# Four U gathers and then the four V gathers of a set, in place of one and one in turn

## The chip, the cores and the metric

The kernel runs on one core of one Trainium2 chip. The metric is the device time of one execution in microseconds (us). A gather here is one indirect DMA of 128 rows of 4 KB, 512 KB in all; U and V are the two expert tables.

## The reference, cut to what matters

One layer: a mixer (an mLSTM and a stick-breaking attention, 4 and 8 heads, over 9 tiles of 128 tokens), then a feed-forward with experts picked by product keys, for 8 tiles of 128 tokens. The gathers serve the second part:

```python
def block(xt):                                   # one tile of 128 tokens
    q = (xt @ w_query).reshape(T, Hh, 2, PEER_HALF)              # Hh = 8 heads
    s = jnp.einsum('thpc,pnc->thpn', q, sub_keys)
    sv, si = lax.top_k(s, K)                                     # K = 16
    cand = (sv[:, :, 0, :, None] + sv[:, :, 1, None, :]).reshape(T, Hh, K * K)
    cidx = (si[:, :, 0, :, None] * N_KEYS + si[:, :, 1, None, :]).reshape(T, Hh, K * K)
    fv, fi = lax.top_k(cand, K)
    eidx = jnp.take_along_axis(cidx, fi, axis=-1)                # 16 of 16384 experts
    g = jax.nn.softmax(fv, axis=-1)
    ue, ve = expert_u[eidx], expert_v[eidx]                      # rows of 1024 floats
    act = jax.nn.gelu(jnp.einsum('td,thkd->thk', xt, ue), approximate=False)
    return jnp.einsum('thk,thkd->td', g * act, ve)
```

So each of 64 heads (8 tiles by 8 heads) needs 16 gathers from `expert_u` and 16 from `expert_v`: 2048 gathers, 1074 MB.

## The kernel before, in words

The first 600 us or so project the tokens and fold the query weights with the keys. Behind that, all engines walk through the same program of slots, 16 slots to a head. In slot `o` of head G each engine does a fixed list, in its own order:

- POOL issues the gathers, and nothing else. `gather_u(G, k)` fetches row k of U for each of 128 tokens into one of 4 ring slots (`RING_U`); before it issues, it waits until VectorE (DVE) has done the dot product that used that ring slot, which is U gather n-4 (`dotted`). `gather_v(G - 1, k)` fetches for the head before into a ring of 8 slots, two sets of four (`SET`); only the first gather of a set waits, for PE to have summed the set two back (`summed_sets`). The V gathers of a head follow one head later since their weights need the finished dots.
- DVE does `dot(G, o)` (L1250) at the start of slot o when U gather o has landed, and after it a part of the routing of a later head: the top 16 of the scores in slots 6, 7, 9 and 10 (`best_halves` L1149 first), the indices in slots 11 to 13; in slots 1 and 2 the weights of the head before; and parts of the mixer of the next tile.
- PE in slots 0, 4, 8 and 12 starts with `sum_set` (16 matmuls, L1351 into `acc`), for the V set of which the last gather was issued just before U gather o. In slot 4, behind it, comes `scores` (16 matmuls, L1351 into `bank` from `n2T`), which `best_halves` in DVE's slot 6 waits for. The mixer's matmuls follow in the same slots.
- ACT copies and does the mixer's and the softmax's exponentials; SP issues plain loads and stores.

An engine can't pass over an instruction that waits: what stands behind it in its program waits too. For DVE that means that a dot stands behind a top-8 that waits for PE, and for POOL that all gathers stand behind one that waits for a dot.

Of the kernel before, what the change touches and what calls it, by code (L numbers as in the profile page):

```python
# [38 lines left out]
PH, TOPK, NKEY = 8, 16, 128  # L39
# [7 lines left out]
SET = 4  # L47
# [20 lines left out]
def wait(eng, sem, value):  # L68

    if isinstance(value, int) and value <= 0:  # L70
        return
    eng.wait_ge(sem, value)
# [17 lines left out]
def tile_of_head(G):  # L90

    return G // PH + 1
# [33 lines left out]
def program(nc, xT, xn_in, w_in, w_out, w_queryT, sub_t, mlstm_w, gain_cols, g_final,  # L126
            gate_bias, expert_u, expert_v, out):
    with ExitStack() as ctx:
# [170 lines left out]
        def b2(i):  # L299
# [6 lines left out]
        COLS = [("u", 0, MIX), ("ks", 2056, MIX), ("qs", 1544, MIX), ("v", 512, MIX),  # L306
                ("so", 1024, MIX), ("vs", 2568, MIX), ("gates", 1536, 2 * MH)]
        w_landed = {n: sem(f"w_landed_{n}") for n, _, _ in COLS}
        x_landed = [sem(f"x_landed{i}") for i in range(2)]
        squared, summed, rs_ready, n_ready = sem("squared"), sem("summed"), sem("rs_ready"), sem("n_ready")  # L310
        unit_done = {n: sem(f"{n}_done") for n, _, _ in COLS}
        unit_taken = {n: sem(f"{n}_taken") for n, _, _ in COLS}
        conv_ready, conv_exp, hist_moved = sem("conv_ready"), sem("conv_exp"), sem("hist_moved")
        staged_act, staged_dve = sem("staged_act"), sem("staged_dve")
# [210 lines left out]
        @block.gpsimd  # L525
        def _(pool):
            def select(tile, sign, op, fill_value):

                pool.affine_select(out=tile[:, :], in_=tile[:, :], compare_op=op, fill=fill_value, base=0,
                                   pattern=[[-sign, P]], channel_multiplier=sign).then_inc(fills, 1)  # L530

            for tile, value in ((ident, 1.0), (ident_h, 1.0), (neg_m, 0.0), (neg_s, 0.0), (before, 1.0),
                                (neg_tri, -1.0), (ones, 1.0), (tri, 1.0), (valid, 1.0),
                                (invalid, 0.0), (eps, EPS), (one, 1.0)):
                pool.memset(tile[:, :], value)
            pool.memset(neg_blk[:, :, :], -1.0)
            pool.memset(lw[:, :], 0.0)
            pool.iota(iota_i[:, :], [[1, TOPK]], base=0, channel_multiplier=0)
            pool.memset(state[:, :, :], 0.0).then_inc(fill, 1)
            pool.wait_ge(fill, 1)  # L540
            select(ident, 1, ALU.is_equal, 0.0)
            select(ident_h, 1, ALU.is_equal, 0.0)
            select(neg_m, -1, ALU.is_ge, NEG)
            select(neg_s, -1, ALU.is_gt, NEG)
            select(before, -1, ALU.is_gt, 0.0)
            select(neg_tri, 1, ALU.is_ge, 0.0)
            select(tri, -1, ALU.is_ge, 0.0)

            pool.affine_select(out=valid[:, :], in_=valid[:, :], compare_op=ALU.is_ge, fill=0.0,
                               base=-(P - N_META), pattern=[[0, 1]], channel_multiplier=1).then_inc(fills, 1)  # L550
            pool.affine_select(out=invalid[:, :], in_=invalid[:, :], compare_op=ALU.is_ge, fill=NEG,
                               base=-(P - N_META), pattern=[[0, 1]], channel_multiplier=1).then_inc(fills, 1)
            pool.affine_select(out=neg_blk[:, :, :], in_=neg_blk[:, :, :], compare_op=ALU.is_equal, fill=0.0,
                               base=0, pattern=[[-1, MH], [0, P]], channel_multiplier=1).then_inc(fills, 1)
            pool.tensor_copy(iota16[:, :], iota_i[:, :]).then_inc(fills, 1)


            def gather_u(G, k):

                T, h = tile_of_head(G), G % PH  # L560
                n = G * TOPK + k
                s = n % RING_U
                wait(pool, dotted, n - RING_U + 1)
                pool.indirect_dma_start(out=ring_u[:, s, :], out_offset=None, in_=expert_u,  # L564
                                        in_offset=bass.IndirectOffsetOnAxis(
                                            ap=chosen[T % 2][:, h * TOPK + k:h * TOPK + k + 1], axis=0)
                                        ).then_inc(u_landed[s], 16)

            def gather_v(G, k):

                T, h = tile_of_head(G), G % PH
                n = G * SET + k // SET
                r, c = k // SET, k % SET
                col = h * TOPK + SET * c + r
                if c == 0:
                    wait(pool, summed_sets, n - 1)
                pool.indirect_dma_start(out=ring_v[:, n % 2 * SET + c, :], out_offset=None, in_=expert_v,  # L577
                                        in_offset=bass.IndirectOffsetOnAxis(ap=idx_v[T % 2][:, col:col + 1], axis=0)
                                        ).then_inc(v_landed[n % 2], 16)

            for G in range(HEADS + 1):
                if G < HEADS:
                    pool.wait_ge(idx_ready, G + 1)
                if G > 0:
                    pool.wait_ge(idx_v_ready, G)
                for k in range(TOPK):
                    if G < HEADS:
                        gather_u(G, k)
                    if G > 0:
                        gather_v(G - 1, k)  # L590


        @block.scalar
# [1107 lines left out]
```

## Time and profile before

| | us |
|---|---|
| median of 3 runs | 3823.41 |
| lowest, highest | 3808.22, 3844.6 |
| profiled execution | 3818.86 |
| its span | 3817.1 |

| engine | busy us | share of the span |
|---|---|---|
| PE | 2173.3 | 57% |
| DVE | 2208.0 | 58% |
| ACT | 614.4 | 16% |
| POOL | 2285.0 | 60% |

The page's part 2 gives the DMA engines as 9 tenths busy or more in nearly every fortieth of the span from 667 us on, and the chain that ended last is POOL for 39%, PE for 19% and DVE for 9%. A share of busy time counts an instruction only while it runs: POOL's time between two gathers isn't in its 60%.

### The profile page before, as it was taken

Reading aid. Unit: us, or ns where it says so; the run is one execution under the profiler, and the core shown is the slowest. Engines: PE = TensorE matmul, PEld = TensorE weight load, DVE = VectorE, ACT = ScalarE, POOL = GpSimd, SP = SyncE. Lnnn points to the kernel's source line nnn. Section 1 sums busy time; section 2 is a strip of 40 time slices with the busy share of each in tenths; the row PEclk is TensorE's granted clock in tenths of the full one; section 3 lists DMA queues with packets and bytes.
Section 4 is the critical chain, followed back from the end, with each engine's and each line's share of the span. In section 5 each row is a group of like instructions: output and inputs, shape, how many; then the busy total and the mean of one; then the engine's idle time right before and its main releaser. Section 6 shows DMA issues by size and latency. Waiting matters only on the chain.

```text
span 3817.1 us, 32434 instructions
## 1 busy us (share of the span) xinstructions
PE 2173.3 (57%) x10710; PEld 1136.1 (30%) x10710; DVE 2208.0 (58%) x5450; ACT 614.4 (16%) x1254; POOL 2285.0 (60%) x2079
## 2 busy tenths in 40 slices
PE   7999864544465445553665457545664477433333
PEld 6777653211232122221332123212321233111100
DVE  2333326666675656665766666657666666666552
ACT  0000122101121112110221023101311132100000
POOL 0000003777677776777677767677677667777675
PEclk9999877765777667666777678766876688666656
DMA  5111414999999999999899989998999899999998
GB/s 178 45 44 38 166 34 137 355 360 374 338 356 339 376 350 346 342 378 348 318 367 374 367 330 345 363 350 323 335 364 374 331 337 362 348 363 369 351 360 315
DMA packets 342724, 1169.34 MB, mean 306 GB/s; under 512 B 37124, under 2 KB 51108, under 8 KB 341544
## 3 DMA queue, kind: packets, MB, share of 16 engines
q0 software_dynamic: 294912, 1073.87, 75.5%
q1 hardware_dynamic: 47656, 93.56, 6.9%
q8 instruction: 77, 1.26, 0.1%
q14 instruction: 79, 0.65, 0.0%
HBM read 1145.25 MB, written 22.04 MB: 306 GB/s over the span
## 4 chain that ended last, share of the span: by engine, by line
POOL 39%; PE 19%; issue 16%; DVE 9%; another core or an unknown queue 8%; DMA 8%; ACT 2%; SPq 0%; POOLq 0%; DVEq 0%; ACTq 0%
POOL work L577 20%; POOL work L564 19%; PE bank L1351 16%; DMA work<-expert_u,chosen 5%; DVE work L1250 3%; PE acc L1351 3%; DMA work<-expert_v,idx_v 2%; DVE work L878 1%; DVE work L886 1%; DVE rest L1153 0%; ACT work L724 0%; ACT work L721 0%; DVE sri L1152 0%; ACT work L728 0%
## 5 line engine op out<-in xcount | busy, mean ns | idle before, releaser
L564 POOL DMA_INDIRECT work<-expert_u,chosen x1024 | 1107.5, 1082 | 1127.4 <-DVE chosen L886 597.5
L1250 DVE CUSTOM_DVE_ANT_0 work<-work,xs 128x1024 f32<-128x1024 f32 x1024 | 1249.3, 1225 | 844.0 <-DMA work<-expert_u,chosen 773.6
L577 POOL DMA_INDIRECT work<-expert_v,idx_v x1024 | 1171.7, 1144 | 388.0 <-issue 308.7
L1351 PE MATMUL acc<-work,lw 128*32 128x512 f32 x4096 | 801.3, 912 | 1013.7 <-DMA work<-expert_v,idx_v 948.2
L1351 PEld LDWEIGHTS acc<-work,lw 128*32 128x32 f32 x4096 | 144.7, 143 | 1419.8 <-DMA work<-expert_v,idx_v 801.1
L1351 PE MATMUL bank<-weights,work 128*128 128x512 f32 x672 | 296.0, 598 | 1.3 <-issue 1.3
L1351 PE MATMUL bank<-weights,n2T 128*128 128x256 f32 x1024 | 256.6, 405 | 1.7 <-issue 1.3
L1351 PE MATMUL bank<-work 64*128 64x128 f32 (+4 forms) x1610 | 212.9, 304 | 50.3 <-DVEq L1178 26.1
L1351 PEld LDWEIGHTS bank<-weights,n2T 128*128 128x128 f32 x1024 | 202.9, 205 | 121.5 <-issue 94.4
L1351 PEld LDWEIGHTS bank<-work 128*128 128x128 f32 (+1 forms) x1610 | 198.6, 211 | 96.9 <-issue 78.3
L1351 PE MATMUL bank<-work,weights 128*128 128x128 f32 x1664 | 192.2, 278 | 3.1 <-DVE work L886 3.1
L1351 PEld LDWEIGHTS bank<-work,weights 128*128 128x128 f32 x1664 | 190.1, 194 | 3.4 <-DVE work L886 3.4
L1351 PE MATMUL bank<-which_eight,c_spread 128*128 128x16 f32 x128 | 33.2, 338 | 264.5 <-DVE c_spread L878 239.3
L1351 PEld LDWEIGHTS bank<-weights,work 128*128 128x128 f32 x672 | 127.4, 192 | 158.8 <-issue 158.4
L1351 PE MATMUL bank<-work,neg_tri 128*128 128x512 f32 x176 | 121.4, 779 | 91.1 <-DVE work L886 65.0
L784 ACT ACTIVATE gate<-best_h,neg_top 128x16 f32<-128x16 f32 x64 | 19.3, 301 | 698.9 <-DVE neg_top L882 642.5
L1351 PEld LDWEIGHTS bank<-which_eight,c_spread 128*128 128x128 f32 x128 | 27.6, 265 | 341.7 <-DVE c_spread L878 293.2
L886 DVE SCALAR_TENSOR_TENSOR work<-work,gains 128x128 f32<-128x128 f32 x180 | 50.5, 346 | 106.4 <-ACT work L614 105.5
L1590 PE MATMUL bank<-ident,w_spread 128*128 128x128 f32 x64 | 25.8, 404 | 140.8 <-DVE w_spread L878 98.0
L886 DVE SCALAR_TENSOR_TENSOR work<-bank,work 128x512 f32<-128x512 f32 x88 | 56.7, 685 | 82.4 <-ACT work L728 61.2
L878 DVE TENSOR_TENSOR work<-work 128x512 f32<-128x512 f32 (+2 forms) x102 | 63.6, 654 | 65.9 <-PE bank L1351 55.0
L1351 PE MATMUL bank<-work,ones 128*128 128x512 f32 (+2 forms) x162 | 100.1, 704 | 0.0
(187 smaller groups left out, 2043.5 us busy)
## 6 DMA issues: line engine op xcount, KB each, us to landing
work<-kv_dram SPq DMA_DIRECT2D x88, 256.0 KB
work<-expert_u,chosen POOLq DMA_INDIRECT x1024
work<-expert_v,idx_v POOLq DMA_INDIRECT x1024
weights<-w_in SPq DMA_DIRECT2D x6, 2048.0 KB, 17.4
mix_dram<-work SPq DMA_DIRECT2D x8, 1024.0 KB, 4.0
weights<-w_queryT SPq DMA_DIRECT2D x4, 2048.0 KB, 17.1
work<-xT SPq DMA_DIRECT2D x9, 512.0 KB, 6.8
kv_dram<-work SPq DMA_DIRECT2D x9, 512.0 KB, 5.7
```

The source lines that it names most:

```text
L564: pool.indirect_dma_start(out=ring_u[:, s, :], out_offset=None, in_=expert_u, in_offset=bass.IndirectOffsetOnAxis(ap=chosen[T % 2][:, h * ...
L577: pool.indirect_dma_start(out=ring_v[:, n % 2 * SET + c, :], out_offset=None, in_=expert_v, in_offset=bass.IndirectOffsetOnAxis(ap=idx_v[T ...
L784: nc.scalar.activation(gate[T % 2][:, a:a + TOPK], best_h[:, :], ACT.Exp, bias=neg_top[:, :], accum_out=gate_sum[T % 2][:, G % PH:G % PH + ...
L878: return nc.vector.tensor_tensor(out_, a, b, op)
L886: return nc.vector.scalar_tensor_tensor(out=out_, in0=a, scalar=s, in1=b, op0=op0, op1=op1)
L1250: nc.vector.tensor_tensor_reduce(s, s, xs[T % 2][:, :], 1.0, 0.0, ALU.mult, ALU.add, dots[:, col:col + 1]).then_inc(dotted, 1)
L1351: return nc.tensor.matmul(out_, lhsT, rhs, start=start, stop=stop, skip_group_check=True)
L1590: nc.tensor.transpose(bank[6][:, 320:448], w_spread[:, :], ident[:, :]).then_inc(w_turned, 1)
```

## The change

In POOL's loop over the heads, the inner loop over the 16 gathers becomes one over four rounds. A round issues four U gathers, then the four V gathers of one set. The number of gathers, their waits' values, the rings and every other engine's program stay.

```diff
-                for k in range(TOPK):
+                for r in range(TOPK // SET):
                     if G < HEADS:
-                        gather_u(G, k)
+                        for k in range(SET * r, SET * r + SET):
+                            gather_u(G, k)
                     if G > 0:
-                        gather_v(G - 1, k)
+                        for k in range(SET * r, SET * r + SET):
+                            gather_v(G - 1, k)
```

POOL's program in the middle of a head, before (`expert_u` and `expert_v` are the tables, `chosen` and `idx_v` the indices, `work` holds both rings):

```order
L564 DMA work<-expert_u,chosen 128x1024 [waits dotted]
L577 DMA work<-expert_v,idx_v 128x1024 [waits summed_sets]
L564 DMA work<-expert_u,chosen 128x1024 [waits dotted]
L577 DMA work<-expert_v,idx_v 128x1024
L564 DMA work<-expert_u,chosen 128x1024 [waits dotted]
L577 DMA work<-expert_v,idx_v 128x1024
L564 DMA work<-expert_u,chosen 128x1024 [waits dotted]
L577 DMA work<-expert_v,idx_v 128x1024
L564 DMA work<-expert_u,chosen 128x1024 [waits dotted,idx_v_ready,idx_ready]
```

The same stretch in the changed kernel, with the round ahead and the first of the next head:

```order
L564 DMA work<-expert_u,chosen 128x1024 [waits dotted] x4
L577 DMA work<-expert_v,idx_v 128x1024 [waits summed_sets]
L577 DMA work<-expert_v,idx_v 128x1024 x3
L564 DMA work<-expert_u,chosen 128x1024 [waits dotted,idx_v_ready,idx_ready]
L564 DMA work<-expert_u,chosen 128x1024 [waits dotted] x3
L577 DMA work<-expert_v,idx_v 128x1024 [waits summed_sets]
L577 DMA work<-expert_v,idx_v 128x1024 x3
```

The waits stay with their gathers. A U gather still stands eight gathers behind the one whose ring slot it takes over; the first V gather of a set, which waits for PE, now stands behind four U gathers of its round in place of one. The last V gather of a set stands right before the next round's first U gather, as it did.

DVE's program is the same before and after. Its slots 5 to 9, with a dot at the start of each (`work,dots<-work,xs`), are in both:

```order
L1250 ISA work,dots<-work,xs 128x1024 [waits u_landed1]
L1250 ISA dots 128x1
L1250 ISA work,dots<-work,xs 128x1024 [waits u_landed2]
L1250 ISA dots 128x1
L1149 MAX srt<-bank 128x8 [waits scores_done]
L1149 MAX srt<-bank 128x8
L1152 MAX_INDEX sri<-srt,bank 128x8 [waits dve_t]
L1153 MATCH_REPLACE rest<-srt,bank 128x128
L1152 MAX_INDEX sri<-srt,bank 128x8
L1153 MATCH_REPLACE rest<-srt,bank 128x128
L878 TENSOR_TENSOR work<-bank,work 128x512 [waits wexp_ready,dve_t]
L1250 ISA work,dots<-work,xs 128x1024 [waits u_landed3]
```

What moves against it is the landing of U: four in a row, then none while four V gathers land.

## Rows read from the trace of the kernel before

**Rows 1.** Who waited for whom on POOL, whole run: total, times, longest

```profile
POOL work L577 <- issue: 308.7, 984, 3.4
POOL work L564 <- issue: 295.6, 946, 1.7
POOL work L564 <- DVE dots L1250: 234.3, 77, 12.7
```

**Rows 2.** The page's part 5: POOL's two groups, busy and mean ns

```profile
L564 POOL DMA_INDIRECT work<-expert_u,chosen x1024 | 1107.5, 1082 | 1127.4 <-DVE chosen L886 597.5
...
L577 POOL DMA_INDIRECT work<-expert_v,idx_v x1024 | 1171.7, 1144 | 388.0 <-issue 308.7
```

**Rows 3.** Four stretches: length, busy time of engines, PE clock, DMA share, GB/s

```profile
660.00:3817.00 3157.00, 1639.65 (x7672) 727.81 (x7672) 1973.47 (x4893) 522.59 (x1067) 2257.00 (x2030) 0.70 0.95 352
...
2425.00:2430.00 5.00, 5.00 (x24) 1.66 (x23) 4.27 (x19) 0.00 (x0) 1.03 (x2) 1.00 0.69 280
...
2465.00:2475.00 10.00, 7.72 (x32) 3.99 (x32) 4.50 (x12) 0.57 (x3) 7.80 (x8) 0.76 1.02 409
...
3500.00:3700.00 200.00, 76.76 (x345) 25.57 (x341) 117.64 (x299) 16.13 (x30) 143.81 (x134) 0.62 0.95 352
```

**Rows 4.** Timeline (start, duration, engine, line): `best_halves`, dots 7 to 13, a gather

```profile
2425.44 0.50 DVE L1149 MAX8 srt<-bank 128x8 f32<-128x128 f32 x2 [6.71 <-remote]
...
2427.16 1.22 DVE L1250 CUSTOM_DVE_ANT_0 work<-work,xs 128x1024 f32<-128x1024 f32 x1
...
2429.64 1.23 DVE L1250 CUSTOM_DVE_ANT_0 work<-work,xs 128x1024 f32<-128x1024 f32 x1 [0.19 <-DVE sri L1162]
2429.91 1.77 POOL L577 DMA_INDIRECT work<-expert_v,idx_v  x1 [0.30 <-issue]
2430.79 1.22 DVE L1250 CUSTOM_DVE_ANT_0 work<-work,xs 128x1024 f32<-128x1024 f32 x1
...
2433.77 1.23 DVE L1250 CUSTOM_DVE_ANT_0 work<-work,xs 128x1024 f32<-128x1024 f32 x1
...
2435.91 1.23 DVE L1250 CUSTOM_DVE_ANT_0 work<-work,xs 128x1024 f32<-128x1024 f32 x1
...
2439.39 1.22 DVE L1250 CUSTOM_DVE_ANT_0 work<-work,xs 128x1024 f32<-128x1024 f32 x1
...
2442.10 1.22 DVE L1250 CUSTOM_DVE_ANT_0 work<-work,xs 128x1024 f32<-128x1024 f32 x1
```

**Rows 5.** Timeline, first and last of 536 pairs: U gather, then its dot

```profile
673.24 0.94 POOL L564 DMA_INDIRECT work<-expert_u,chosen  x1 [0.30 <-issue]
...
679.23 1.23 DVE L1250 CUSTOM_DVE_ANT_0 work<-work,xs 128x1024 f32<-128x1024 f32 x1 [0.88 <-DMA work<-expert_u,chosen]
...
3771.62 1.00 POOL L564 DMA_INDIRECT work<-expert_u,chosen  x1 [0.31 <-issue]
...
3778.22 1.23 DVE L1250 CUSTOM_DVE_ANT_0 work<-work,xs 128x1024 f32<-128x1024 f32 x1 [1.29 <-DMA work<-expert_u,chosen]
```

**Rows 6.** Timeline, first and last of 61 heads: dot 4, then `best_halves`

```profile
677.12 1.22 DVE L1250 CUSTOM_DVE_ANT_0 work<-work,xs 128x1024 f32<-128x1024 f32 x1
...
686.75 0.49 DVE L1149 MAX8 srt<-bank 128x8 f32<-128x128 f32 x2
...
3654.74 1.23 DVE L1250 CUSTOM_DVE_ANT_0 work<-work,xs 128x1024 f32<-128x1024 f32 x1 [1.29 <-DMA work<-expert_u,chosen]
...
3662.25 0.50 DVE L1149 MAX8 srt<-bank 128x8 f32<-128x128 f32 x2 [1.16 <-PE bank L1351]
```

**Rows 7.** Timeline, PE: one `sum_set`, and one `scores`

```profile
2411.01 3.64 PE L1351 MATMUL acc<-work,lw 128*32 128x512 f32 x16 [3.25 <-DMA work<-expert_v,idx_v]
...
2414.58 4.02 PE L1351 MATMUL bank<-weights,n2T 128*128 128x256 f32 x16
```

**Rows 8.** Timeline, POOL: a U gather of the first head

```profile
621.66 4.83 POOL L564 DMA_INDIRECT work<-expert_u,chosen  x1 [12.70 <-DVE dots L1250]
```

**Rows 9.** Groups by line: `best_halves`' first operation; busy, mean ns, idle before it

```profile
L1149 DVE MAX8 srt<-bank 128x8 f32<-128x128 f32 x128 | 31.6, 288 | 101.4 <-remote 71.2 <-PE bank L1351 29.9 <-issue 0.2
```

## The prediction

> **What bounds the kernel now.** I read POOL first, since all traffic behind 600 us starts there. Its waits [rows 1] and its two groups [rows 2] add up: 1107.5 + 1171.7 = 2279 us of gathers, 309 + 296 = 604 us of gaps of 0.30 us between them, and 234 us in which a U gather waits for a dot. That is 3117 of the 3157 us behind 660 us [rows 3]. So POOL is never free, though the page calls it 60% busy.
>
> A gather needs 0.94 us where nothing is in its way [rows 5], with the gap 1.24. The means are 1.08 and 1.14 [rows 2]. The excess, 2279 - 2048 x 0.94 = 354 us, comes from DVE's dots: a V gather that starts 0.27 us into a dot takes 1.77 us [rows 4], 0.83 more, which is the rest of that dot, and it gets in between this dot and the next, that follows without a gap. I call this the lock.
>
> Are the DMA engines the limit? They moved 352 GB/s over the long stretch, but 409 over 10 us in which POOL ran freely, and 280 after a stall of POOL [rows 3]. A gather costs them 0.524 MB / 409 = 1.28 us, POOL 1.24: close, but POOL's delays decide.
>
> From the start of a U gather to its dot, where DVE stood waiting, it takes 6.25 us: the median of 536 pairs, of which the first and last have 5.99 and 6.60 [rows 5].
>
> One head takes (3771.62 - 673.24) / 1002 x 16 = 49.5 us [rows 5]: 32 x 1.24 = 39.7 bare, 354/64 = 5.5 lock, 234/64 = 3.7 waits for dots, the rest for V.
>
> **The change, part by part.** No gather, byte or instruction is added. What changes is when U lands: four in about 5 us, then none for 5 us, where it was one each 3.1 us. The distance from a U gather to the reuse of its slot stays eight gathers. Four terms follow.
>
> (a) The wait of a V set for PE is looser by three gathers. It was nearly nothing; I give 0.6 us a head for it, from the rest in the account above.
>
> (b) The tail. The last U gather is issued three gathers earlier, 3.7 us once. Left out.
>
> (c) The lock. In a burst of light slots dots follow landings at 1.24 to 1.28 us, about POOL's own step, so after one collision (0.6 us on average, half a dot) POOL falls into the gaps. Where slots carry routing, dots stand 2 to 3 us apart and each meets a gather again.
>
> (d) The scores. This is what turns it. PE starts `sum_set` of slot 4 when the last V of the set has landed, just before U4 lands in both orders; then come `scores`. In one head they took 3.64 + 4.02 = 7.7 us [rows 7]. `best_halves` starts 9.63 us after dot 4 in the first head and 7.51 in the last [rows 6]; over 61 heads the mean is 9.0, the median 8.4. Before, U7 lands 9 us after U4, so dot 7 behind `best_halves` is about on time. Now U7 lands 3.8 us after U4, and its dot must still wait for 9.0 + 1.72 = 10.7 us (1.72 is from `best_halves` to dot 7 [rows 4]). The U gather that needs dot 7's slot, U11, is due at POOL some 8 us after U4 has landed, and is held back, with four V gathers behind it.
>
> Worked through for a head, with U4 issued at time 0, landing 6.25 after issue, DVE's steps from dot to dot as [rows 4] has them (slot 7 2.48, slot 8 1.15, slot 9 2.98, slot 10 2.14, slot 12 2.71 us) and 1.24 a gather:
> - U4 to V7: 0 to 9.9, one collision, so U8 at 10.6, U9 11.8, U10 13.1; U11 would be at 14.3.
> - `best_halves` at 6.25 + 9.0 = 15.25, dot 7 at 17.0, done 18.2; U11 at 18.4: 4.1 us late.
> - DVE: dots 8, 9, 10, 11 at 19.45, 20.6, 23.6, 25.7. V8 starts at 19.7 and is locked to 20.55, V9 21.8, V10 23.0, V11 24.3 locked to 24.7, U12 26.0 locked to 26.8.
> - U13 to V15: 28.1 to 35.5. Dots 12 to 15 at 33.05, 35.8, 37.5, 38.7. U16 36.9, U17 locked to 38.6, U18 39.9, U19 41.1, V16 42.3, V17 locked to 44.25, V18 locked to 46.0, V19 47.3, U20 48.5.
>
> So 48.5 us a head: 39.7 + 4.1 late + 4.7 lock. Before, the same account has 39.7 + 5.5 and the waits. Two things must be added. Of the 234 us of waits for dots (3.7 a head) a part is term (d) in its old size, and the rest comes from the mixer's work and stays. No row parts them; with all of it (d) nothing is added, with none 3.7. I take half, 1.9. And the mixer now meets a DVE that does its first slots of a round close together, sooner than PE can answer: between nothing (if every such wait falls into the pause behind the round's last dot) and 1.8 us a head. The upper end is the mixer's own DVE work taken whole: DVE is busy for 0.625 of the long stretch and for 0.588 of 200 us in which no mixer runs [rows 3], and 0.037 x 49.5 = 1.8. I take 0.7, nearer to nothing, since each round has 5 us of pause. 48.5 + 1.9 + 0.7 = 51.1, against 49.5: **+1.6 us a head**. (a) is already in it, since 48.5 has no V wait.
>
> 63 heads have both kinds: 63 x 1.6 = 101 us. On the profiled execution's own time, 3818.9 (the span and 1.8 around it, and 4.5 under the median of the runs), that gives 3920 us, 2.6% more.
>
> **A rule that speaks against any change.** The 10 us at 409 GB/s [rows 3] say that the memory can give more than the mean of 352. The Trainium skill, "DMA: Bandwidth & Descriptors", Specifications, puts the limit of HBM for one core at about 358 GB/s. By that rule the kernel would stand at the limit, and the order of gathers would be worth nothing: 3820 us. The trace doesn't agree in a short stretch; it doesn't show a long one.
>
> **The rivals.**
> - *Slower by the late dot 7*, as above: 0.62.
> - *No change*, since the DMA engines are the true limit and POOL's delays only follow. For it: a DMA share of 0.95 [rows 3]. Against it: bytes and share both fall after a stall of POOL (280 GB/s, 0.69), and free gathers take 0.94 with no back-pressure. Within 1%, around 3820; together with the case that terms (c) and (d) cancel: 0.23.
> - *Faster by the lock.* If the dots of all rounds fall into POOL's step, the lock is 4 x 0.8 = 3.2 us a head, not 5.5, and the V wait goes. That decides where `best_halves` starts less than some 5.6 us after U4 lands: then dot 7 isn't late. It would give 39.7 + 3.2 + 3.7 = 46.6, 2.9 us less a head, 3636 us; with half of it 3730. For it: PE's granted clock averages 0.70 [rows 3], between its levels of 1.2 and 2.4 GHz, so the two steps are shorter in some heads than the 7.7 us of [rows 7]. Against it: a mean of 9.0 over 61 heads. 0.13.
> - *POOL starved.* One gather took 4.83 us with three dots behind each other running [rows 8]. If a burst of four dots kept POOL out for its whole length, each round would cost 4 x 1.15 - 0.6 = 4 us more: 252 rounds, 1000 us, 4900 us. Against it: the V gather at 2429.91 that got in between two such dots [rows 4]. 0.02.
>
> **How the numbers follow.** Each us of `best_halves`' start is one us a head, 63 us in all. With the median 8.4 the forecast is 3882; with 7.0, 3794. With the mixer's 1.8 whole it is 3920 + 69 = 3989, and with two thirds of the 1.8 that the halved 3.7 leaves open on top, 4065. The likeliest case alone spans 3790 to 4065. The whole range reaches a little into the faster case: 3770 to 4065. About 1% is what a measurement of this kernel tells from no change. Faster by over 1%: 0.13; within: 0.23; slower, the starved case with it: 0.64.
>
> **What would show it.** POOL's waits for dots should grow from 234 us to some 450, in more than 100 waits, and most of them at U11; its two groups should fall from 2279 us together to about 2230 (4.7 against 5.5 of lock). DVE's wait of L1149 for PE [rows 9] should grow from 101 us to over 250. DMA bytes stay and the mean falls from 352 to about 342 GB/s. Wrong if L1149 waits longer and L564 doesn't: then dot 7 has slack that I don't see. Wrong too if the mean gather grows past 1.2 us: that would be the lock, not the scores.

## The result, and the profile after

The changed kernel takes 3956.8 us, the median of four runs (3947.1 to 3962.0), against 3827.2 for the kernel before in the same comparison: a ratio of 1.034, 95% interval 1.028 to 1.039. The profiled execution has a span of 3952.9 us, 135.8 more than before (3817.1). The forecast was 3920 us, slower, by the late dot 7.

POOL's waits in the kernel after (who waited for whom: total, times, longest), against [rows 1]:

```profile
POOL work L564 <- DVE dots L1252: 465.8, 123, 12.7
POOL work L577 <- issue: 309.5, 1015, 0.3
POOL work L564 <- issue: 287.0, 900, 2.1
POOL work L577 <- PE acc L1353: 9.9, 6, 4.7
POOL work L577 <- remote: 7.4, 3, 3.8
```

Two waits of the kernel before that [rows 1] doesn't have, the V gathers' for `sum_set`:

```profile
POOL work L577 <- remote: 68.9, 34, 3.4
POOL work L577 <- PE acc L1351: 10.4, 6, 3.6
```

POOL's two groups in the page's part 5 of the kernel after (busy, mean ns, idle time ahead of them), against [rows 2]:

```profile
L564 POOL DMA_INDIRECT work<-expert_u,chosen x1024 | 1077.4, 1052 | 1348.4 <-DVE chosen L888 595.7
...
L577 POOL DMA_INDIRECT work<-expert_v,idx_v x1024 | 1177.3, 1150 | 326.8 <-issue 309.5
```

The first operation of `best_halves` in the kernel after, by line, against [rows 9], and the long stretch, against [rows 3]:

```profile
L1151 DVE MAX8 srt<-bank 128x8 f32<-128x128 f32 x128 | 31.8, 290 | 233.2 <-remote 143.3 <-PE bank L1353 73.2 <-issue 16.7
```

```profile
660.00:3952.00 3292.00, 1643.94 (x7665) 728.15 (x7664) 1957.43 (x4890) 520.10 (x1065) 2232.59 (x2030) 0.69 0.91 337
```

(Lines behind the change are two higher than before: L1250 is now L1252.) POOL's groups give the whole account. U gathers: idle ahead of them 1348.4 against 1127.4, that is +221.0; V gathers: 326.8 against 388.0, -61.2; busy time 2254.7 against 2279.2, -24.5. The sum is +135.3, for 135.8 of span. The waits for dots grew by 231.5 us; the V gathers' waits for `sum_set`, 79 us before (the page calls most of them "remote"), fell to 17. The DMA engines' share fell from 0.95 to 0.91 and the rate from 352 to 337 GB/s: they have more idle time, so they are not what bounds the changed kernel.

Sorted by the U gather that waits, and counted over the usual gap of 0.30 us (my sums from the timeline), U11 waited 62.7 us in 23 heads before and 212.8 us in 53 heads after. The others together, the first head's among them, went from 148.5 to 216 us. Most of that rise stands in few heads: U10 50.9 us in 10 heads (28.1 in 9 before), U6 23 in 8 (2 before), U2 19 in 7 (0.4 before), those of U10 and U2 all one to three heads into a tile of eight (heads 1, 2, 9, 10, 17, 18, 19 and so on).

One round of the changed kernel shows it step by step. This is its timeline in an execution on another chip (the run after2, below): start, duration, engine, line.

```profile
2512.06 0.94 POOL L564 DMA_INDIRECT work<-expert_u,chosen  x1 [0.30 <-issue]
...
2522.06 0.94 POOL L564 DMA_INDIRECT work<-expert_u,chosen  x1 [0.30 <-issue]
2524.80 0.94 POOL L564 DMA_INDIRECT work<-expert_u,chosen  x1 [1.81 <-DVE dots L1252]
2526.05 0.94 POOL L577 DMA_INDIRECT work<-expert_v,idx_v  x1 [0.30 <-issue]
```

```profile
2517.23 1.23 DVE L1252 CUSTOM_DVE_ANT_0 work<-work,xs 128x1024 f32<-128x1024 f32 x1
...
2521.58 0.50 DVE L1151 MAX8 srt<-bank 128x8 f32<-128x128 f32 x2 [3.12 <-PE bank L1353]
...
2523.30 1.23 DVE L1252 CUSTOM_DVE_ANT_0 work<-work,xs 128x1024 f32<-128x1024 f32 x1
```

```profile
2513.20 3.64 PE L1353 MATMUL acc<-work,lw 128*32 128x512 f32 x16 [6.76 <-DMA work<-expert_v,idx_v]
2516.78 4.77 PE L1353 MATMUL bank<-weights,n2T 128*128 128x256 f32 x16
```

U7 is issued at 2512.06. In this run a dot for which DVE stood waiting starts 6.45 us after its gather (median of 269), so U7's rows land near 2518.5, just as dot 6 (2517.23) ends. But PE began `sum_set` only at 2513.20 and the scores end at 2521.55. `best_halves` starts at 2521.58 and dot 7 at 2523.30, some 5 us after its data. U11, due at 2523.3 as well, must wait for the end of that dot and goes out at 2524.80, with four V gathers behind it.

### The profile page after: what moved, and what is told of

Read it like the earlier page. It is cut to its first block, busy times and chain, and to the rows that moved or that the text cites. A ratio compares the mean times of both kernels' runs of the same rounds, so it can differ in the third digit from the quotient of the medians.

```text
span 3952.9 us, 32434 instructions
## 1 busy us (share of the span) xinstructions
PE 2176.9 (55%) x10710; PEld 1135.8 (29%) x10710; DVE 2194.1 (56%) x5450; ACT 613.4 (16%) x1254; POOL 2260.5 (57%) x2079
## 4 chain that ended last, share of the span: by engine, by line
POOL 31%; PE 23%; issue 13%; DVE 12%; DMA 12%; another core or an unknown queue 7%; ACT 3%; SPq 0%; POOLq 0%; DVEq 0%; ACTq 0%
PE bank L1353 18%; POOL work L577 17%; POOL work L564 13%; DMA work<-expert_v,idx_v 6%; DVE work L1252 6%; DMA work<-expert_u,chosen 6%; PE acc L1353 5%; DVE work L880 1%; DVE rest L1155 1%; DVE sri L1154 1%; DVE srt L1151 1%; DVE work L888 1%; ACT work L726 0%; ACT work L723 0%
## 5 line engine op out<-in xcount | busy, mean ns | idle before, releaser
L564 POOL DMA_INDIRECT work<-expert_u,chosen x1024 | 1077.4, 1052 | 1348.4 <-DVE chosen L888 595.7
L1252 DVE CUSTOM_DVE_ANT_0 work<-work,xs 128x1024 f32<-128x1024 f32 x1024 | 1242.4, 1223 | 794.5 <-DMA work<-expert_u,chosen 730.3
L577 POOL DMA_INDIRECT work<-expert_v,idx_v x1024 | 1177.3, 1150 | 326.8 <-issue 309.5
L1353 PE MATMUL bank<-weights,n2T 128*128 128x256 f32 x1024 | 267.5, 418 | 1.3 <-issue 0.8
L1353 PEld LDWEIGHTS bank<-weights,n2T 128*128 128x128 f32 x1024 | 211.1, 213 | 124.7 <-issue 94.6
L1151 DVE MAX8 srt<-bank 128x8 f32<-128x128 f32 x128 | 31.8, 290 | 233.2 <-remote 143.3
L738 ACT ACTIVATE work<-bank 128x512 f32<-128x512 f32 x88 | 52.3, 597 | 380.2 <-PE bank L1353 260.3
```

The lines of the kernel that those rows point to most:

```text
L738: nc.scalar.activation(zl[hg], bank[2 + hg][:, :], ACT.Exp).then_inc(a_ready, 1)
L1151: last = nc.vector.max(values[:, 0:8], src)
L1252: nc.vector.tensor_tensor_reduce(s, s, xs[T % 2][:, :], 1.0, 0.0, ALU.mult, ALU.add, dots[:, col:col + 1]).then_inc(dotted, 1)
L1353: return nc.tensor.matmul(out_, lhsT, rhs, start=start, stop=stop, skip_group_check=True)
```

## The experiments

Each run stands beside the kernel before on its own chip, and three chips were met: A, where before takes 3799 us, B with 3647 and C with 3645. So ratios are compared, and traces only of one chip; where a comparison crosses chips, I say so. Which chip the result was taken on isn't known. The kernel before took 3827 us there and DVE's waits look like A's (last section), so the traces of the result are set beside A's. X is the mean time from the start of dot 4 to that of `best_halves` over 60 heads, from the timelines.

### The cost of the scores itself

a_few, in `scores`, chip A:

```
-                for k in range(KC):
+                for k in range(2):
...
-                              w_score[:, 2 * h:2 * h + 2, k, :], k == 0, k == KC - 1)
+                              w_score[:, 2 * h:2 * h + 2, k, :], k == 0, k == 1)
```

> The changed kernel with 4 of the 16 matmuls of scores (2 of 8 parts of the sum over the model's width are computed, the other 6 left out, so other experts are picked, as many as before). Scores are ready up to 3 us earlier, best_halves stays in slot 6. Late-dot-7 theory: each us is a us a head while dot 7 is late, about 50 heads: U11's waits fall from 213 to some 80 us, the time to 3800 to 3850 us. DMA theory: 3940 to 3970 us.

Measured: 3822.3 us, 1.005 (1.001 to 1.009). X fell from 8.8 to 6.5 us, U11's waits from 212.8 to 123.7 us. POOL in a_few:

```profile
POOL work L564 <- DVE dots L1252: 340.2, 105, 8.9
```

The kernel leaves out three quarters of the scores' matmuls, and the time came as the theory says; U11's waits fell less than to its 80 us. The direction fits over three runs of this order (two chips): X is 8.8, 7.0 and 6.5 us, and U11 waits 213, 121 and 124 us. Yet that alone doesn't say that the order makes them dear. The control is b_few, the same edit in the kernel before, chip B.

> The kernel before, with 4 of the 16 matmuls that make a head's scores (so the scores are incomplete); it is the control for the same cut in the changed kernel, which brought that one from 3957 to 3822 us. Theory (the late scores cost time through the order of the gathers, since dot 7 holds back U11 with four V gathers behind it): in the order before they cost little, so this gives 3760 to 3800 us, 0 to 40 us less than before, dotted waits from 234 to about 170 us. Rival (PE's work for the scores costs the same whatever the order of the gathers, by its clock or its place on the chain): a gain of 100 us or more here too, below 3700 us.

Measured: 3592.6 us, 0.983 (0.979 to 0.986); waits for dots 94.5 us in 49. That is between theory and rival: the kernel before pays 1.7% for its scores too, more than I had given it. The cut takes 2.9 points from the changed kernel and 1.7 from the one before (on different chips), so some 1.1 of the 3.4 points are the scores made dearer by the order. That is a difference of four measured times; their intervals together leave it open by about 0.7 either way. What stands between the two with few scores is still 2.3 points.

### best_halves behind dot 7

a_late moves two steps of `routing` in the changed kernel, chip A; b_late does it in the one before.

```
-                if o == 6:
+                if o == 7:
                     best_halves(G)
-                if o == 7:
+                if o == 8:
                     next_halves(G)
```

> The changed kernel, with DVE's best_halves moved from slot 6 to slot 7, so behind dot 7, the last of its round, and next_halves to slot 8. PE and the gathers stay. Late-dot-7 theory: U11 no longer waits for a dot that stands behind the wait for the scores; its 213 us of waits go nearly whole, POOL's waits for dots fall from 466 to under 280 us, and the time from 3957 to 3740 to 3800 us. DMA theory (bursts of U feed the 16 engines worse): nothing changes there, 3940 to 3970 us. Mixer theory (the waits come from the mixer's ping-pong with PE): at most a fifth of the 130 us comes back, 3925 us or more.

> The kernel before, with the same move of best_halves to slot 7 and next_halves to slot 8. Late-dot-7 theory: the waits of U10 to U12 (110 us of 234) shrink but less is to be had than in the changed kernel: 3750 to 3800 us from 3827. If the move helps for another reason that has nothing to do with the order of gathers (DVE waits less for PE in all), it gives the same number of us in both kernels.

Measured: a_late 3926.2 us, 1.032 (1.028 to 1.036), a miss; b_late 3797.8, 0.998 (0.993 to 1.002), no gain. In b_late POOL's waits for dots are 190.1 us, 44 less than before, but its waits of L577 are 103.4, 24 more. In a_late U11's waits fell from 212.8 to 46.5 us as foretold, but U12 to U15 rose to 250 us in 103 waits:

```profile
POOL work L564 <- DVE dots L1252: 487.0, 163, 12.7
```

The lateness was passed on, not removed. On chip A a second thing confuses the picture: waits of up to 12 us at MAX8 (last section). So I ran the edit again on chip C, with a small memset between the wait and MAX8, as a_late2, beside after2, which is the changed kernel unaltered.

> The changed kernel again, unaltered, so that the other three stand beside it on the same chip; chips differ (the kernel before took 3799 us on one and 3647 us on another). 1.034 of the time of before if the cost of the order doesn't hang on the chip; 1.04 if the faster chip, which loses less elsewhere, shows it more.

> The changed kernel with best_halves in slot 7 and next_halves in slot 8, as in the run that gave 1.032, and with the memset of 8 columns between the wait for the scores and MAX8. Theory (dot 7 ahead of best_halves frees U11; what spoiled it in the first run were waits of 5 to 12 us for scores that PE had finished, which the faster chip doesn't show): 1.00 to 1.02 there, with U11's dotted waits under 20 us. Rival (the lateness only passes to dots 8 to 11 and so to U12 to U15, on any chip): 1.03 again. On a chip with the long waits: if they stand ahead of the memset, PE's signal is late; if ahead of MAX8, it is MAX8 that can't start.

Measured: after2 3789.8 us, 1.039 (1.036 to 1.042); a_late2 3749.3, 1.029 (1.026 to 1.031). Chip C has no long waits, X is 6.95 for after2, and the order costs no less. POOL's waits for dots in after2, then in a_late2:

```profile
POOL work L564 <- DVE dots L1252: 322.9, 127, 12.6
```

```profile
POOL work L564 <- DVE dots L1253: 362.5, 173, 12.6
```

POOL's groups in after2, then in a_late2:

```profile
L564 POOL DMA_INDIRECT work<-expert_u,chosen x1024 | 1087.9, 1062 | 1192.4 <-DVE chosen L888 595.6
...
L577 POOL DMA_INDIRECT work<-expert_v,idx_v x1024 | 1164.7, 1137 | 321.3 <-issue 310.5
```

```profile
L564 POOL DMA_INDIRECT work<-expert_u,chosen x1024 | 1051.0, 1026 | 1223.5 <-DVE chosen L888 598.1
...
L577 POOL DMA_INDIRECT work<-expert_v,idx_v x1024 | 1121.2, 1095 | 320.0 <-issue 309.9
```

The waits for dots went up, from 322.9 to 362.5 us: U11 fell from 120.6 to 37.9, U14 and U15 rose from 35.8 to 131.5. The gain of 50 us is in the other column: 80 us less busy time of POOL. In after2 649 gathers took over 1.00 us, in a_late2 503, so fewer met a dot; a_late, without the memset, has 70 us less busy time than the kernel after, and b_late only 6 less than the one before. The rival is right on the waits, on both chips: `best_halves` then stands ahead of dots 8 to 11, which are drawn together as well.

### The fifth slot

a_ring5 in the changed kernel, chip A (the last gain is left out to make room):

```
-RING_U = 4
+RING_U = 5
```

> The changed kernel with 5 U ring slots in place of 4. Room for it comes from leaving out the final gain: the output is scaled by itself instead, same operation and size, and one load of 512 KB at the start is gone. U11 then needs dot 6, which stands ahead of best_halves, and U12 needs dot 7. Late-dot-7 theory: the waits at U11 go, some come back at U12; POOL's waits for dots under 200 us, 3700 to 3800 us. DMA theory: a gather more in flight, at most 20 to 40 us less.

Measured: 3832.9 us, 1.009 (1.005 to 1.013), less gain than expected. Waits for dots are still 330.4 us in 128, now the most at U12 (89.2), the gather that needs dot 7's slot in a ring of five. The control b_ring5, chip B:

> The kernel before with five U slots in place of four, the last gain left out to make room (the output is scaled by itself in its place); it is the control for the same change of the changed kernel, which came to 3833 us. Theory (the ring of U binds POOL only where the order puts four U gathers behind a late dot): the order before needs the fifth slot less, some 50 to 100 of the 234 us of dotted waits go, 3700 to 3770 us. Rival (POOL's own issue of 1072 gathers, or the transfer rate, is what bounds both): 3780 to 3800 us, with the time that leaves the dotted waits found in other waits of POOL or in longer gathers.

Measured: 3593.5 us, 0.984 (0.982 to 0.987), waits for dots 65.1 us in 23. The theory's 3700 to 3770 us were written for chip A; as shares of before they are 0.974 to 0.992, and that held. A fifth slot gives the changed kernel 2.5 points and the one before 1.6. So it brings the orders only from 3.4 to 2.4 points apart (on different chips, and open by about 0.7 either way). The fifth slot doesn't take the late dot away: in the changed kernel dot 7 now holds back U12. This run alone doesn't say how large its part is. POOL's waits in b_ring5:

```profile
POOL work L562 <- DVE dots L1248: 65.1, 23, 12.0
```

### How large, and where, the groups are

a_two, chip B: in POOL's loop, groups of two U and two V gathers.

```
-                for r in range(TOPK // SET):
+                for r in range(TOPK // 2):
...
-                        for k in range(SET * r, SET * r + SET):
+                        for k in range(2 * r, 2 * r + 2):
```

> The changed kernel with groups of two: two U gathers, then two V gathers, and so on. Theory (what costs is how many U gathers in a row need slots whose dots come late): a U gather behind dot 7 now has two V gathers behind it, and the cost lies between the two orders: 3850 to 3900 us where four give 3957 and one gives 3800; dotted waits about 340 us. Rival (any grouping upsets the stream by the same amount): 3930 to 3960 us. Second rival (the cost comes only of four in a row, a whole ring): 3790 to 3820 us.

Measured: 3682.0 us, 1.009 (1.006 to 1.013), waits for dots 180.2 us in 80, of which U11 49.2. The theory's 3850 to 3900 us are 1.013 to 1.027 of chip A's before, so the cost is a little under its range and above that of the second rival: it grows faster than the group. A group of four is also a whole ring of U; no run parts the two. POOL's waits in a_two:

```profile
POOL work L564 <- DVE dots L1252: 180.2, 80, 12.7
```

a_shift, chip C: groups of four, moved by two.

```
-                for r in range(TOPK // SET):
+                for r in range(TOPK // SET + 1):
                     if G < HEADS:
-                        for k in range(SET * r, SET * r + SET):
+                        for k in range(max(SET * r - 2, 0), min(SET * r + 2, TOPK)):
                             gather_u(G, k)
-                    if G > 0:
+                    if G > 0 and r < TOPK // SET:
```

> The changed kernel with the groups of four moved by two: U0 and U1, V set 0, U2 to U5, V set 1, U6 to U9, V set 2, U10 to U13, V set 3, U14 and U15, then the next head. Theory (dots 4 to 7 of one group are drawn together to 1.3 us apart, and the scores, best_halves and dot 7 don't shrink with them, so that dot 7 is late for U11): now the pause between two groups falls between dots 5 and 6, where the scores are worked out anyway, so most of the cost goes: 0.99 to 1.01 of the time of before, dotted waits under 300 us, U11 under 30 of them. Rival (grouping in fours costs by itself, wherever it falls): 1.025 to 1.04 as after. Second rival (it only moves to the next routing step, next_halves in slot 7 and the join in slot 8, now in the middle of a burst): 1.015 to 1.03, with the waits at U12 and U13.

Measured: 3708.4 us, 1.017 (1.015 to 1.020), more than the theory's 0.99 to 1.01, though its two marks came (198.6 us of waits for dots; U11 10.5). Groups of the same size, put so that the pause between two of them falls where the scores are worked out, cost 1.7% in place of 3.9: a little over half of the cost hung on where the bursts fall, and U11's waits alone fell by more (120.6 to 10.5 us) than the span did (84.8 us). The rest is what the second rival named, now small waits over many gathers (U12 33.5 us in 39), and in longer gathers:

```profile
POOL work L564 <- DVE dots L1252: 198.6, 131, 12.6
```

```profile
L564 POOL DMA_INDIRECT work<-expert_u,chosen x1024 | 1094.6, 1069 | 1074.0 <-DVE chosen L888 595.5
L577 POOL DMA_INDIRECT work<-expert_v,idx_v x1024 | 1197.0, 1169 | 317.1 <-issue 311.4
```

### Scores ahead of sum_set

b_swap in the kernel before, chip C: PE does the scores first in slot 4.

```
+                    if o == 4 and 0 <= I - ROUTE < HEADS:
+                        scores(I - ROUTE)
                     if o % SET == 0 and 0 <= v < SETS:
                         sum_set(v)
...
-                        if o == 4:
-                            scores(I - ROUTE)
```

> The kernel before with PE doing a head's scores ahead of the sum_set that stood in front of them, so that they end some 2 to 3.6 us earlier. It is the one edit here that might beat both kernels with the output whole. Theory (dot 7's deadline has slack in the order before, and lateness of the scores still costs part of the dotted waits): 0.99 to 1.00 of the time of before, dotted waits down by 20 to 60 us, best_halves 2 us earlier after dot 4. Rival (sum_set later by 4 us makes a V slot late, and so POOL's V gathers): 1.00 to 1.01, with waits of L577 on PE acc up by 30 us or more.

Measured: 3621.9 us, 0.994 (0.991 to 0.996): faster than both kernels, with the output whole. POOL's waits and groups in b_swap:

```profile
POOL work L564 <- DVE dots L1250: 105.2, 60, 12.7
POOL work L577 <- PE acc L1351: 23.0, 16, 4.1
```

```profile
L564 POOL DMA_INDIRECT work<-expert_u,chosen x1024 | 1080.7, 1055 | 996.1 <-DVE chosen L886 597.4
L577 POOL DMA_INDIRECT work<-expert_v,idx_v x1024 | 1173.0, 1145 | 338.2 <-issue 315.2
```

It also gives a clean account on one chip. Between b_swap and after2 lie 177.9 us of span: U gathers' idle time +196.3, V gathers' -16.9, busy time -1.1. Of the waits for dots, U11 gives 114 us (120.6 against 6.8) and U10 38. (b_swap isn't the kernel before; that one takes 23 us more on this chip, and no trace of it there was taken.)

### What a late MAX8 waits for

a_probe is the changed kernel with a memset between the wait for the scores and MAX8, one execution on chip B:

```
                 dve.wait_ge(scores_done, G + 1)
+                nc.vector.memset(srt[:, 1, 8:16], 0.0)
```

> The changed kernel with one more DVE instruction per head between the wait for the scores and the first MAX8: a memset of 8 columns of the list that MAX8 writes next. In the kernel after, 23 or so of these waits last over 3 us though PE's last scores matmul has ended in the records. If PE's signal comes late (first theory), the memset takes over the long waits and MAX8 follows it within 0.3 us. If it is MAX8 that can't start while POOL issues gathers (second theory), the memset starts when the signal comes, within 1.3 us of the last matmul, and the long waits stand ahead of MAX8. The time stays at 3930 to 3970 us by both.

Measured: 3798.2 us, one execution, 1.04 of its before. It settles nothing on the long waits, since chip B showed none. It couldn't have parted the two theories by the place of the wait either. The memset stands ahead of MAX8 in the program, but in the trace it starts 0.01 us behind it, and all 51 waits (135.0 us) are put down to MAX8:

```profile
789.47 0.28 DVE L1151 MAX8 srt<-bank 128x8 f32<-128x128 f32 x1 [1.89 <-issue]
789.48 0.07 DVE L1175 MEMSET srt<- 128x8 f32 x1
```

The last matmul of these scores ends at 789.42; in all 51 waits MAX8 starts within 0.1 us of it.

## Why the prediction was right

The step that turned it, (d), was right in place and nearly in size. It put U11 4.1 us late in each head; measured are 212.8 / 64 = 3.3, and 4.0 in each of the 53 heads where it waits. The groups of four moved by two took U11's waits away, and over half of the cost with them. The cost came out at 135.8 / 64 = 2.1 us a head, where 1.6 had been forecast. In the prediction's own terms, before and after:

| us a head | forecast | measured |
|---|---|---|
| POOL's waits for dots | 3.7 to 6.7, +3.0 | 3.3 to 6.7, +3.4 |
| (a), V's waits for PE | 0.6 to 0, -0.6 | 1.2 to 0.2, -1.0 |
| (c), the lock | 5.5 to 4.7, -0.8 | 5.5 to 5.1, -0.4 |

The rows add up to +1.6 and +2.0. The errors of the first two cancel, which is luck, and the lock is what is left of the miss. Where each came from:

- U11: 4.1 foretold, 3.3 measured. `best_halves` started 8.8 us after dot 4, not 9.0, and some ten heads have no such wait. The good match is partly luck of the chip: on chip C, where no MAX8 is late, U11 waits 120.6 / 64 = 1.9 us a head and the order costs no less.
- All other waits for dots: 1.9 + 0.7 = 2.6 us a head foretold, 216 / 64 = 3.4 measured, which makes up for U11. The 1.9, a half of the old waits taken for want of a row, stood for what was 148.5 / 64 = 2.3, and the mixer's 0.7 for a rise of 68 us, 1.1. The rise stands mostly in few heads, while the routing has its steps in every head; that the mixer makes it is likely but not shown.
- (a): the prediction took it from the rest of its account of a head, where it came out too small. The 39.7 us already hold the usual gap of 0.30 us ahead of every gather, and the 234 us of waits for dots hold it again, 77 times. Over that gap they are 211 us, and the V gathers' waits 76.
- (c): small, in the right direction, and not fixed by the order: a_late2 shows 80 us less of it. Gathers of over 1.00 us went from 708 to 652.
- The signs: waits for dots 465.8 us in 123 (some 450, over 100), of which U11 is about half and not most; both groups 2254.7 us (about 2230); DVE's wait at L1151 233.2 us (over 250); DMA rate 337 GB/s (342).

The rival that the DMA engines are the limit is out. So is the rule that went with it, which the prediction took as a limit of this core. The Trainium skill ("DMA: Bandwidth & Descriptors", Specifications) gets its about 358 GB/s of HBM for one core by halving a stack's 716 between two cores. This kernel runs on one core, and the trace doesn't agree with 358 as its limit: chip C moved 377 GB/s over 2940 us in b_swap:

```profile
660.00:3600.00 2940.00, 1625.50 (x7658) 749.17 (x7660) 1970.06 (x4889) 518.70 (x1060) 2229.93 (x2030) 0.73 0.99 377
```

There its DMA share is 0.99, so this kernel is now close to both limits, POOL's and the engines'. b_few and b_ring5 are there too (380 and 381 GB/s, share 0.99, from 660 to 3500 us), so the controls in the old order may have had less left to gain than the runs that they stand beside.

Of the whole cost I call this shown: about half hangs on where the bursts fall, with U11's waits behind `best_halves` and its scores as what goes when they are moved (a_shift: 2.1 of 3.9 points). The other half came with grouping in fours even then. The whole grows with the size of the group (0.9 points for two, 3.4 to 3.9 for four). How that other half divides into waits of single steps and locked gathers wasn't parted. Two things would tell more and weren't run: the scores ahead of `sum_set` (b_swap's edit) in the changed kernel, and a trace of the kernel before on chip B or C.

## What to carry to other kernels

Grouping issues for one consumer draws its work together, while the steps that another engine feeds into the same stretch keep their length; so ask of each slot of the ring when its reader must be done, measured in issues of the new order, and what stands between that reader and its data. Where such a step is late, look first at its place against the burst: in the changed kernel a_shift took off 2.1 points, moving the step one slot back 1.0 (a_late2), with longer waits at the next gathers. The producer's own order is worth a trial too: b_swap took 0.6 points off the kernel before, where one slot back (b_late) took nothing clear of noise. And give an ablation its control in the old order: the cut scores looked like the whole answer until the kernel before gained 1.7% by them too.

## What the runs showed of the hardware

Chips differ by 4% in this kernel: 3799, 3647 and 3645 us for the same program. On chip A, and in the executions of the comparison of the result, DVE waits at MAX8 with nothing near that the trace could name, long after PE's last scores matmul. In the kernel after, timeline of PE, DVE and POOL:

```profile
2191.10 3.84 PE L1353 MATMUL bank<-weights,n2T 128*128 128x256 f32 x16
```

```profile
2199.95 0.50 DVE L1151 MAX8 srt<-bank 128x8 f32<-128x128 f32 x2 [6.62 <-remote]
```

```profile
2196.92 0.94 POOL L564 DMA_INDIRECT work<-expert_u,chosen  x1 [0.30 <-issue]
2203.17 0.94 POOL L564 DMA_INDIRECT work<-expert_u,chosen  x1 [5.32 <-DVE dots L1252]
```

The scores end at 2194.94 and MAX8 starts 5.0 us later, 2.1 us after POOL's last gather ended. PE was idle from the end of its scores on. V gathers show such waits for `sum_set` too (the 68.9 us called "remote" before), as if PE's signals came late. Loaded DMA engines alone don't do it: chip B moved 380 GB/s in b_few, and shows none. In the kernel after the page calls 24 waits at MAX8 "remote", 143 us; on chips B and C there is none, and after2 waits 128.8 us there, all for PE within the reach of its matmuls:

```profile
L1151 DVE MAX8 srt<-bank 128x8 f32<-128x128 f32 x128 | 31.7, 289 | 128.8 <-PE bank L1353 128.8
```

They go with the slower chip, and don't explain the difference between the orders: that is 3.4% with them and 3.9% without. Counted from the end of PE's last scores matmul, MAX8 starts late by 89 us in all in the kernel before and by 98 us in the one after. Their cause is open: the memset meant to find it ran only on chips that don't show them.
